# Pre-norm scale moved from the operands to the matmul results in a four-layer transformer kernel

## The reference

```
h = rms_norm(x, pre)            # x * rsqrt(mean(x*x) + 1e-6) * weight, mean over channels
x = x + rms_norm(mixer(h) @ w_out, post)
h = rms_norm(x, pre_ffn)
x = x + rms_norm(ffn(h), post_ffn)
```

## Time and profile before

| | |
|---|---|
| median of 3 runs | 3311.93 us (3303.95 to 3357.27) |
| the profiled execution | 3332.28 us, span 3330.6 us |
| TensorE matmuls | busy 94% of the span |
| VectorE, ScalarE, GpSimd | busy 36%, 35%, 41% |
| mean granted TensorE clock | 0.936 of full speed |
| chain of waits that ended last | TensorE 73%, issue 17%, GpSimd 5%, VectorE 2%, ScalarE 1% |
| weight loads | 398 x 512 KB, 3.3 us to landing; memory traffic 65 GB/s on average |

### The profile page before, as it was taken

How to read it: one execution, slowest core, us unless ns; L and a number is a source line. 1 busy time by engine, 2 the same in 40 slices (tenths; PEclk the granted TensorE clock), 3 DMA queues, 4 the chain that set the end, 5 groups by cost and what they waited for, 6 DMA issues and landing times.

```text
span 3330.6 us, 45326 instructions
## 1 busy us (share of the span) xinstructions
PE 3117.0 (94%) x14204; PEld 2443.5 (73%) x14204; DVE 1213.3 (36%) x2281; ACT 1154.2 (35%) x1799; POOL 1366.5 (41%) x722
## 2 busy tenths in 40 slices
PE   6989998999899899899998999989998998989998
PEld 4778786888677787688885467768886556768886
DVE  3445424441243553344303584130012467330012
ACT  3342334443324423444323222343333223343232
POOL 3432135555444211455545240255554432155564
PEclk8999989999999998999999885889999988989999
DMA  2220011233212000122331120012222111012222
GB/s 102 83 70 1 1 46 62 94 101 101 79 65 87 26 1 1 59 99 94 101 101 54 44 70 1 32 61 97 95 99 75 51 50 40 26 63 95 95 95 94
DMA packets 58776, 217.32 MB, mean 65 GB/s; under 512 B 6576, under 2 KB 6704, under 8 KB 58384
## 3 DMA queue, kind: packets, MB, share of 16 engines
q1 hardware_dynamic: 58320, 214.48, 19.4%
q0 software_dynamic: 320, 1.12, 0.1%
HBM read 213.48 MB, written 2.10 MB: 65 GB/s over the span
## 4 chain that ended last, share of the span: by engine, by line
PE 73%; issue 17%; POOL 5%; DVE 2%; DVEq 1%; ACT 1%; ACTq 0%; DMA 0%; POOLq 0%
PE bank L1409 63%; POOL hL L565 3%; PE bank L1500 2%; PE bank L1511 2%; PE bank L1466 1%; POOL eb L582 1%; PE bank L1529 1%; PE bank L1474 1%; PE bank L1520 1%; PE bank L1486 1%; POOL x L578 1%; PE bank L1435 1%; DVE sc L1328 0%; PE bank L1457 0%; DVE x L1018 0%
## 5 line engine op out<-in xcount | busy, mean ns | idle before, releaser
L556 POOL TENSOR_TENSOR wL<-raw,wH 128x1024 fp32r<-128x1024 f32 x398 | 958.6, 2409 | 1114.7 <-ACT wH L680 1114.7
L1409 PE MATMUL bank<-hH,wH 128*128 128x512 f32 x2256 | 933.1, 414 | 78.4 <-POOL hL L565 77.3
L1409 PE MATMUL bank<-hL,wH 128*128 128x512 f32 x2256 | 894.9, 397 | 0.0
L1409 PE MATMUL bank<-hH,wL 128*128 128x512 f32 x2256 | 894.2, 396 | 0.0
L1409 PEld LDWEIGHTS bank<-hH,wH 128*128 128x128 f32 x2256 | 431.3, 191 | 248.8 <-POOL hL L565 112.1
L1409 PEld LDWEIGHTS bank<-hH,wL 128*128 128x128 f32 x2256 | 433.7, 192 | 94.4 <-issue 12.8
L1409 PEld LDWEIGHTS bank<-hL,wH 128*128 128x128 f32 x2256 | 432.7, 192 | 92.6
L680 ACT ACTIVATE wH<-raw 128x1024 fp32r<-128x1024 f32 x398 | 419.4, 1054 | 231.9 <-PE bank L1409 214.6
L1409 PE MATMUL bank<-hidH,wH 128*128 128x512 f32 x864 | 339.6, 393 | 0.0
L1409 PE MATMUL bank<-hidH,wL 128*128 128x512 f32 x864 | 336.4, 389 | 0.0
L1409 PE MATMUL bank<-hidL,wH 128*128 128x512 f32 x864 | 336.4, 389 | 0.0
(11 more groups left out here) (254 smaller groups left out, 3419.7 us busy)
## 6 DMA issues: line engine op xcount, KB each, us to landing
raw<-w_dram SPq DMA_DIRECT2D x398, 512.0 KB, 3.3
x<-x_dram SPq DMA_DIRECT2D x4, 512.0 KB, 9.1
out_dram<-x SPq DMA_DIRECT2D x1, 2048.0 KB, 6.2
const<-const_dram SPq DMA_DIRECT2D x1, 1421.5 KB, 12.8
par_next<-par_dram POOLq DMA_DIRECT2D x5, 168.0 KB, 2.6
posi<-pos_dram POOLq DMA_DIRECT2D x1, 256.0 KB, 7.0
const<-const_dram SPq DMA_DIRECT2D x1, 130.5 KB, 2.2
```

What stands on the lines that cost most here:

```text
L556: pool.tensor_tensor(wL[:, s, :], raw[:, s, :], wH[:, s, :].bitcast(F32), ALU.subtract).then_inc(w_lo.sem, 1)
L1409: mm = pe.matmul(ACC[bk][:, :], wt[:, s, c:c + P], rhs, start=first and k == 0 and j == 0, stop=last and k == tiles - 1 and j == 2)
```

## The change

- hH and hL are made from `x * weight` without rstd: ScalarE writes hH directly (`norm`), VectorE writes hL (`low`); GpSimd and the ring of pieces have no part in it. The residual runs tile by tile on VectorE, with `low` of the tile before behind each tile.
- The first unit of a stage (`first_unit`) follows these tiles; TensorE sums the squares of each tile behind it, with tokens in partitions. The root and its reciprocal give `rtok`; TensorE spreads it behind the fifth tile of unit 1 (`norm_scale`), ScalarE copies it to `rstd`.
- Results are multiplied by rstd: by scaled rotation tables (`norm_scales`), by VectorE on the result in its bank or out of it (`unit_scaled`), by `rtok` in the transposed values, in the gates' copy, and in the FFNs' evacuation.
- Of the output norm, the last square is summed by TensorE itself; the wH conversion of the last output unit moves behind the root; the roots need no table load between them.
- The trigonometry stands inside the first projection (units 1 and 2 of the first layer).
- ScalarE, VectorE and GpSimd have the layers written out one after another instead of in a loop; TensorE and the load queue keep their loops.

```diff
-            def norm(w, r0, half, n0, x0):
+            def norm(w, half):
...
+                if half == 0:
+                    act.wait_ge(par_loaded.sem, par_loaded.at(w, 16))
                 for k in range(KD):
-                    act.wait_ge(x_ready[k % 2].sem, x_ready[k % 2].at(w, x0 // 2 + k // 2 + 1))
+                    act.wait_ge(x_ready.sem, x_ready.at(w, KD * (half - 1) + k + 1))
+                    act.activation(hH[:, k, :], x[:, k, :], ACT.Copy,
+                                   scale=pre_weight(w, half, k)).then_inc(h_high.sem, 1)
                     square(w, r0 + k, k % 2, x[:, k, :])
-                act.activation(rstd[:, :], STAT[:, :], ACT.Ln, bias=cst("eps"),
-                               scale=1.0 / D).then_inc(stat_free.sem, 1)
-                use_table("exp_and_others")
-                act.drain()
-                act.activation(rstd[:, :], rstd[:, :], ACT.Exp, scale=-0.5).then_inc(rstd_ready.sem, 1)
-                if half == 0:
-                    narrow_gates(w)
-                for k in range(KD):
-                    piece_high(w, n0 + k, (n0 + k) % 2, hH[:, k, :])
+                act.wait_ge(sq_used.sem, sq_used.at(w, r0 + KD))
+                act.activation(root[:, 0, 0:NT], STAT[:, 0:NT], ACT.Sqrt, bias=cst("eps"),
+                               scale=1.0 / D).then_inc(norm_root.sem, 1)
+                if half == 0:
+                    use_table(EXP)
+                    act.activation(par[:, :], par_next[:, :], ACT.Copy).then_inc(par_in.sem, 1)
+                    narrow_gates(w)
+                act.wait_ge(norm_spread.sem, norm_spread.at(w, half + 1))
+                act.activation(rstd[:, :], STAT[:, :], ACT.Copy).then_inc(rstd_ready.sem, 1)
...
+            def low(w, half, k):
+                dve.wait_ge(h_high.sem, h_high.at(w, KD * half + k + 1))
+                dve.scalar_tensor_tensor(hL[:, k, :], x[:, k, :], pre_weight(w, half, k), hH[:, k, :].bitcast(F32),
+                                         ALU.mult, ALU.subtract).then_inc(h_low.sem, 1)
...
+            def residual(w, half, name, after):
...
                 for k in range(KD):
+                    dve.scalar_tensor_tensor(m[:, k, :], m[:, k, :], prm(w, name, k, k + 1), R1[:, :],
+                                             ALU.mult, ALU.mult)
+                    dve.drain()
+                    dve.tensor_tensor(x[:, k, :], x[:, k, :], m[:, k, :], ALU.add).then_inc(x_ready.sem, 1)
+                    if after and k:
+                        low(*after, k - 1)
...
+            def first_unit(w, i2, s, bk, a2, half):
...
+                for k in range(KD):
+                    c = k * P
+                    pe.wait_ge(h_high.sem, h_high.at(w, KD * half + k + 1))
+                    pe.matmul(ACC[bk][:, :], wH[:, s, c:c + P], hH[:, k, :], start=k == 0, stop=False)
+                    pe.matmul(ACC[bk][:, :], wL[:, s, c:c + P], hH[:, k, :], start=False, stop=False)
+                    pe.wait_ge(h_low.sem, h_low.at(w, KD * half + k + 1))
+                    mm = pe.matmul(ACC[bk][:, :], wH[:, s, c:c + P], hL[:, k, :], start=False, stop=k == KD - 1)
...
+                    add_token_sums(STAT, sq[:, k % 2, :], k == 0, k == KD - 1).then_inc(sq_used.sem, 1)
...
+                    if k == 4 and scale is not None:
+                        norm_scale(w, scale)
...
+            def unit_scaled(w, u, out, sem):
+                dve.wait_ge(unit_done.sem, unit_done.at(w, u + 1))
+                dve.tensor_tensor(out, ACC[u % 2][:, :], rstd[:, :], ALU.mult).then_inc(sem, 1)
...
+                            dve.wait_ge(unit_done.sem, unit_done.at(w, i * 4 + 37 + 2 * q + s))
+                            dve.tensor_tensor(ACC[s][:, :], ACC[s][:, :], rstd[:, :],
+                                              ALU.mult).then_inc(acc_scaled.sem, 1)
...
-                            act.activation(relu[:, s, :], ACC[bk][:, :], ACT.Relu).then_inc(acc_free[bk].sem, 1)
+                            act.activation(piece[:, s, :], relu[:, s, :], ACT.Square).then_inc(piece_ready.sem, 1)
+                            act.activation(hidH2[:, bass.ds(i * 2 + s, 1), :], relu[:, s, :],
+                                           ACT.Square).then_inc(piece_hi.sem, 1)
                             next_high(w, i + 15 + 16 * c, s)
-                            piece_high(w, N_HID2 + HCH * c + i * 2 + s, s, hidH2[:, bass.ds(i * 2 + s, 1), :])
...
-                            dve.tensor_tensor(piece[:, s, :], relu[:, s, :], relu[:, s, :],
-                                              ALU.mult).then_inc(piece_ready.sem, 1)
+                            dve.scalar_tensor_tensor(relu[:, s, :], ACC[bk][:, :], 0.0, rstd[:, :], ALU.max,
+                                                     ALU.mult).then_inc(acc_free[bk].sem, 1)
```

## The result

The changed kernel takes 3365.77 us (median of 20 runs, 3330.3 to 3405.55). Measured beside it, the kernel before takes 3339.03 (20 runs, 3298.14 to 3388.11). The ratio is 1.010, 95% interval 1.006 to 1.015: about 1% slower. Ratios here compare fast runs alone, those not over 1.5% above the fastest of their kernel, while medians are of all runs. I had forecast 3264 with a range of 3224 to 3302. The profile shown first here is of the slowest of the 20 runs; the second is of a run of 3369.69, and the passages of both agree within 1.3 us.

The account below looks back on a forecast made before the run. TensorE, busy 94%, was taken as the bound, idle mainly in passages between stages. Savings of 77.5 us less losses of 11, 4, 6 and 8 gave -48.5: 3283.8 us, on the median 3264, range 3224 to 3302.

Parts of the forecast that it names:

- The failed step: First unit's tiles: TensorE's 1.73 us a tile, token sums included, stays hidden below VectorE's 2.08 at the high clock.
- My own list of signs: Signs of being wrong: tiles 3 us apart, no wait before unit 2, units 5.44 apart, PSUM-input VectorE operations over 0.8 us.
- Entries: Unit 2 starts earlier: four FFN entries 32.4 us, first block's layer entry 13.4, second block's two 12.8, start 18.9; sum 77.5.
- (a): Second block's FFN, 64 units: relu and two squares make the next weights 0.46 us late; 11 us lost (0 to 19).
- (b): First block's FFN, 88 units: a VectorE product ahead of the activation makes every second unit later; 4 us lost (0 to 8).
- (c): Second block's pool units: the copy out of the bank moves from ScalarE to VectorE; 6 us lost (3 to 10).
- (d): Clock: new idle stretches of 2 to 4.2 us in the passages cost 1 us for each of eight; 8 us (0 to 20).
- base of 3311.93: Median of the kernel before's runs, in us, to which the forecast was scaled from the profiled execution's 3332.28.
- The low clock follows each new wait: Rival: the clock term at 20 us and the start's saving only 11; 3284 us, chance 0.12.
- The slower rival: In both blocks' FFNs VectorE's new products wait for GpSimd, 92 us more; 3355 us, 1.3% slower, chance 0.06.

Follow-up runs that it names:

- e1_after: The changed kernel run again unchanged for a second profile; median 3360.94 us, ratio to the kernel before 1.010.
- e6: Changed kernel with unit 2's weights made early, weights ahead of the squares, and one ones-matrix sum per tile in four FFN entries; 3220.94 us, ratio 0.969.
- e10: Changed kernel with the ones-matrix sum in the four FFN entries as its only edit; 3306.81 us, ratio to the kernel before 0.996.
- e9: e6's kernel with the ones-matrix sum in the layer entries too, so in all eight first units; 3259.96 us, ratio to the kernel before 0.984.
- e7: Changed kernel with early unit 2 weights, weights ahead of the squares, and a useless 512-column matmul behind tiles 0 to 6 of first units; 3293.56 us, ratio 0.990.
- e12: Kernel before with useless one-column, 512-column or 128-column matmuls behind each tile of nine units of the first block's projection; one run, 3667.2 us.
- e3: Changed kernel with the high part of the next weights made ahead of the two squares in the second block's FFN; 3321.11 us, ratio 0.998.
- e15: Changed kernel with 16 keep-warm calls ahead of the first block's mixers; 3318.34 us, ratio to the kernel before 1.001.
- e13: e9's kernel with 16 keep-warm calls ahead of the first block's mixers; 3259.02 us, ratio to the kernel before 0.977.
- e11: Kernel before with 16 keep-warm calls ahead of the first block's mixers; 3342.37 us, ratio to the kernel before 1.004.

## Why the prediction was wrong

By its profile (e1_after against the kernel before, ends of the last stage 3343.8 and 3307.2), the 36.6 us are: first block's mixers +44.0, FFN stages +35.4, start to the first mixer -10.8, second layer's entry and projection -5.9, second block's layers -26.1. In terms of the clock: 97 us more at the low clock in the passages, 42 us by the slope; 45 more in the mixers, 19 us; the rest, -24, is what the change gives at an equal clock. The medians agree: at an equal clock 3118 for the changed kernel and 3143 for the one before, -25. I had forecast -56.5 apart from the clock and +8 for it.

- **The failed step** is "TensorE's share of a tile, 0.68 + 1.05 = 1.73, is hidden below 2.08 at the high clock", together with the remark that tiles keep TensorE at 83% until the wait. I priced the token sums by their 1.05 us from the earlier trace rows, where eight of them stand alone, and never asked what 64 of these instructions among a unit's 24 matmuls do to the clock. What the runs show in its place: the clock falls to 0.50 some 11 to 14 us behind T0, a tile then takes 2.99 us of TensorE, and unit 1 starts at T0+28.6 to T0+29.5. Shown by e6 and e10 (replace the sums in the FFN entries, and unit 1 is at T0+23.06), by e9 (the same at the layer entries and the start), by e7 (filling the idle time does not help) and by e12 (twice as many drop it without any idle time). My own list of signs named it: "tiles 3 us apart (TensorE at the low clock...)".
- **Entries.** Unit 2 gained 0.2, -0.8, 1.5 and 0.3 us in the FFN entries (forecast 8.1 each), 5.6 in the layer entry (13.4), -1.9 and 2.5 in the second block's entries (6.4 each), and 10.5 at the start (18.9; with TensorE low throughout I had 11): 18 us in place of 77.5. At the start it is the same step again: I had some 4 us at the low clock, and with the token sums it was 29; e9, without them, rises after 4.5 us. The base of the forecast was off as well: the FFN entries of the second block had unit 2 at T0+43.6 before, not at 42.2, and the last layer's entry at T0+51.9, not at 48.25, so by my own steps these three had 1.4, 1.4 and 3.7 us more to give. The steps up to the fourth tile held within 0.3 us, the wait for unit 2's weights was 4.23 (4.2), that for the narrow weights 3.4 (3.6).
- **(a)** was right in its mechanism and too small: 5.62 + 5.88 = 11.50 for two units against 5.48 + 5.75, so 0.31 a unit and some 20 us for 64 units, just past the end of my range (19). e3 took 21 of it back at an equal clock.
- **(b)** 4.3 us in each of the two stages behind the sixth unit, 8.6 in all: mis-sized at 4, just past its upper end, 8. **(c)** TensorE waits 5.4 us for the pool units' banks, forecast 6.
- **(d)** The clock was given 8 us for the waits, with an end at 20. The waits' share was of that order (each is followed by some 6 us at 0.50, 2.5 us by the slope, so 10 for the four FFN entries), but the tiles and the mixers were not in the term at all.
- **The rivals.** On the base of 3311.93 the change came out at 3311.93 x 1.0104 = 3346. "The low clock follows each new wait", at 3284, was the nearest in its mechanism, and 62 us short. The slower rival, at 3355, was the nearest in its number, by luck: its mechanism, VectorE's products waiting for GpSimd, did not occur. The taps took 749 ns in 176 cases again, and the relu product 692. Its sum was also wrong: two units at 12.5 in place of 11.23 are 41 us more for 64 units, not 52, since the 11 of (a) was in already; that gives 3344.
- **What I left out.** The mixers. Both profiles of the kernel before show them at 272.2 us with a clock of 0.91, and its own runs spread by 2.7% (3298 to 3388). Such a spread on one core was to be read as a clock that hangs on small things. e15 shows that for the changed kernel alone 0.9% hangs on it, as much as the whole measured loss. The same 16 calls moved e9's kernel and the one before by nothing clear (e13, e11), so they are no cure, and what in them does it is not shown: the later begin and the keep-warm work itself were not separated.

Whether the change is slower "in itself" has therefore no one answer. With its own mixers it loses 1.0%; with 3.7 us of keep-warm ahead of them it is level. In both the passages cost it some 42 us that the sum did not have. Not settled: why one kernel's mixers fall and another's don't, and 9 of the 31 us between -56.5 and -25; (a) and (b) explain 14, and the start, where the 29 us at the low clock aren't counted, 8.

## What to carry to other kernels

Price a matmul by what it does to the clock of its neighbours, not only by its own duration: sums over partitions that are taken column by column, interleaved with dense matmuls, halved the speed of the dense ones, and the same sum as one 512-column matmul with a matrix of ones left the clock at 1.00. When a conversion for a later unit (weights) has no need of a statistic, put it ahead of the wait for the statistic. And before a result of 1% is put down to a change, look at the stages it does not touch: here they moved by as much as the whole result, and 3.7 us of keep-warm matmuls in front of them moved them back.

## What the hardware showed that I had not expected

- The granted clock fell from 1.00 to 0.50 within 4.5 us, and stayed there for 102.8 us, while TensorE was busy for every us, when eight one-column matmuls (16 instructions) stood behind every three of 512 columns; it held with eight of 128 columns or two of 512 in their place (e12_probe, one run). The Trainium skill ("TensorE: Matmul & The Clock Gate", section "HAM oscillation — how this bites in real kernels") puts falls of the clock down to gaps in which TensorE is idle. The trace of this case shows such falls too (551.20 to 556.90, behind the 4.23 us wait), but the tiles fell with gaps of 0.4 us at most, and the probe with none.
- A reciprocal of 128x512 on VectorE takes 3352 ns, against 178 for 128x4 (e6_ones_sum, four cases). In the second block's FFN entries it fits in unit 1, 5.44 us long. In the first block's it is on the way to unit 0's bank: it ends at 532.70, VectorE's product on the bank starts at 532.97, and unit 2 starts at 536.39 behind a wait of 2.35 us, T0+31.4 in place of 28.9.
- A keep-warm call is two instructions of 0.117 us each: 16 calls took 3.73 us.
